# Delta rule over the prompt: where the second key unit of the next head stands on TensorE

## The chip, the cores and the metric

The kernel runs as one program on one core of a Trainium2 chip. The metric is the device time of one execution in microseconds (us). Three runs of the kernel before took 2859.43, 2862.31 and 2866.95 us; their median is 2862.31 us. A change of 0.3% is about 8.6 us.

## The reference

The program is one decoder layer: adaptive norm, one input projection, a gated delta rule, a sliding-window attention, two gates, an output projection and a mixture of experts. The change lies in the delta rule over the 1024 prompt tokens, 8 heads of width 128. The reference computes for each head, in chunks of 64 tokens:

```python
A = where(strict, (k * beta) @ k.T * decay, 0)
L = A + eye(C)
sol = triangular_solve(L, [v * beta, k * beta * exp(gc)])
u, w = sol[..., :DV], sol[..., DV:]
# chunk by chunk, S starts at 0
v_new = u - w @ S
o = q_dec @ S + (q @ k.T * decay) @ v_new
S = S * g_end + k_dec.T @ v_new
```

The q, k and v that enter are columns of one product of the normed input with `w_in`, passed through a causal convolution of four taps, SiLU and (q and k) a norm.

## The kernel before, in words

`delta_prompt` (L422) walks over the eight heads in a hardware loop: seven passes with a next head (`nxt` is true) and a last one without. Here a chunk is 128 tokens, so a head has eight, and they are handled as two groups `g` of four. All eight chunk matrices are inverted before the state is touched.

Projections. Each head needs four projections: q (t = 0), k (1), v (2) and the output gate z (3). One is made in three units of 352 columns, and `project(t, u, half, j)` (L880 to L896) makes half of one unit for head `j`: 12 products, so a unit is 24. The 24 write one PSUM bank: `gd_ps` for units 0 and 2, `gd_pv` for unit 1. Units 0 and 2 first wait until ScalarE has copied out what the bank held before; unit 1 waits only for its weights. The q and k units of head i+1 are made while head i is in its solve, and serve as filling for TensorE.

The solve. VectorE inverts the 16x16 diagonal blocks of all chunks by itself (`solve`, L766), which takes about 7 us. SyncE writes the blocks to a scratch in device memory and reads them back in the layout of whole chunk matrices, `gd_Y` and its transpose `gd_YT`, one group after the other. Three levels follow, `l` = 4, 5 and 6, each of which joins blocks of twice the size:

- TensorE multiplies (`gd_x<-gd_Y,gd_am`, L915; at level 6 `gd_Y,gd_AT`, L984), once for each group. This is the level's first product.
- ScalarE copies the result out of PSUM as `gd_T` (L685, L687).
- TensorE multiplies by `gd_YT` (`gd_x<-gd_T,gd_YT`, L915; at level 6 L1006). This is the second product.
- VectorE subtracts from `gd_Y` (L823; at level 6 from a corner of `gd_YT`, L836).
- For levels 5 and 6 TensorE first turns the new `gd_Y` over (L927) behind the first product, and VectorE copies it to `gd_YT` (L826).

What sets the order. Every engine has its own instruction list, written out by hand, and executes it in order; semaphores join the lists. On TensorE (`body`, L930 on) the list of a head in this stretch is: q unit 0, the turn of k, q units 1 and 2, k unit 0 (the loop over `m`, L968), level 4, the first products of level 5, half of k unit 1, the second products of level 5, the other half of k unit 1, then level 6 with the halves of k unit 2 in the same places, then the products with `gd_k` (L915) and the loop over the chunks, where the z units of the next head are the filling. VectorE has in its list, between the `gd_YT` copies of level 4 and the subtractions of level 5, two taps of the q convolution of the next head (`conv(0, i + 1, 2, CONV)`, L753). ScalarE copies k unit 1 out (L611) behind the two `gd_T` copies of level 5. The last head has no next one, and so no projections in its list.

Of the kernel before, what the change touches and what calls it, by code (L numbers as in the profile page):

```python
# [421 lines left out]
def delta_prompt(nc, c, w_in, gdn_norm, out_state):  # L422
# [10 lines left out]
    with ExitStack() as ctx:  # L433
# [47 lines left out]
        def split_count(t, j):  # L481

            return j * 4 + (RANK[t] + 1)
# [25 lines left out]
        with nc.Block() as block:  # L509
# [365 lines left out]
            def _(pe):  # L875
                def passes(t, n, at):

                    return ((half_of(t)[:, n, :], hh[:, n, at]), (half_of(t)[:, n, :], hl[:, n, at]), (w_r[t][:, n, :], hh[:, n, at]))

                def project(t, u, half, j):  # L880

                    done = (qk_proj, qk_proj, v_proj, z_proj)[t]
                    dst = pp[u % 2] if t == 3 else (pps, pv, pps)[u]
                    dst, at = dst[:, 0:C3], slice(u * C3, (u + 1) * C3)
                    if half == 0:
                        pe.wait_ge(w_low, split_count(t, j))
                        m = t * 3 + u
                        if t < 2 and u != 1:
                            pe.wait_ge(qk_evac, j * 6 + m - u // 2)
                        if t >= 2 and u == 2:  # L890
                            pe.wait_ge(v_evac if t == 2 else z_evac, j * 3 + 1)
                    for n in range(4 * half, 4 * half + 4):
                        for v, (a, b) in enumerate(passes(t, n, at)):
                            last = nc.tensor.matmul(dst, a, b, start=(n == 0 and v == 0), stop=(n == KD - 1 and v == 2))  # L894
                    if half == 1:
                        last.then_inc(done, 1)  # L896
# [15 lines left out]
                def quad(dst, a, b):  # L912
                    for n in range(4):
                        at = slice(n * P, (n + 1) * P)
                        last = nc.tensor.matmul(dst[:, at], a[:, at], b[:, at], start=True, stop=True)  # L915
                    return last

                def turn(dst, a, g):
                    for n in range(4):
                        at = slice((4 * g + n) * P, (4 * g + n + 1) * P)  # L920
                        last = nc.tensor.transpose(dst[:, n * P:(n + 1) * P], a[:, at], c.ident[:])
                    return last

                def turn_tiles(dst, a):
                    for n in range(4):
                        at = slice(n * P, (n + 1) * P)
                        last = nc.tensor.transpose(dst[:, at], a[:, at], c.ident[:])  # L927
                    return last

                def body(i, nxt):  # L930
# [34 lines left out]
                        pe.wait_ge(ats, i * 8 + g * 4 + 4)  # L965
                        turn(X[g][0], y[1], g).then_inc(turned, 1)
                    if nxt:
                        for m in range(1, 4):  # L968
                            for half in range(2):
                                project(m // 3, m % 3, half, i + 1)  # L970
                    for l in (4, 5, 6):
                        for g in range(2):
                            if l == 4:
                                pe.wait_ge(kts, i * 2 + g + 1)
                                pe.wait_ge(y_in[g], i * 32 + 32)
                            else:
                                pe.wait_ge(ys, i * 4 + (l - 5) * 2 + g + 1)
                            if l < 6:
                                pe.wait_ge(lvl, i * 4 + (l - 4) * 2 + g + 1)
                                quad(X[g][0], am[g][l % 2], Y[g]).then_inc(p1, 1)  # L980
                            else:
                                for n in range(4):
                                    lo, hi = slice(n * P, n * P + HP), slice(n * P + HP, (n + 1) * P)
                                    last = nc.tensor.matmul(X[g][0][:, lo], AT[g][0:HP, n * P:(n + 1) * P], Y[g][0:HP, lo], start=True, stop=True)  # L984
                                last.then_inc(p1, 1)
                            if l == 5:
                                pe.wait_ge(qds, i * 4 + g * 2 + 2)
                            if l > 4:
                                turn_tiles(X[g][1], Y[g]).then_inc(yturned, 1)
                        if l == 4:  # L990
                            pe.wait_ge(v_silu, i + 1)
                            pe.wait_ge(capped, i * 8 + 8)
                            for g in range(2):
                                turn(pp[g], y[2], g).then_inc(vturned, 1)
                        elif nxt:
                            project(1, l - 4, 0, i + 1)
                        for g in range(2):
                            pe.wait_ge(t1, i * 6 + (l - 4) * 2 + g + 1)
                            if l > 4:
                                pe.wait_ge(yts, i * 6 + (l - 5) * 2 + g + 1)  # L1000
                            if l < 6:
                                quad(X[g][0], YT[g], T1[g]).then_inc(p2, 1)
                            else:
                                for n in range(4):
                                    lo, hi = slice(n * P, n * P + HP), slice(n * P + HP, (n + 1) * P)
                                    last = nc.tensor.matmul(X[g][1][:, hi], T1[g][HP:P, n * P:(n + 1) * P], YT[g][HP:P, hi], start=True, stop=True)  # L1006
                                last.then_inc(p3, 1)
                        if nxt and l > 4:
                            project(1, l - 4, 1, i + 1)
                    for g in range(2):  # L1010
                        pe.wait_ge(yts, i * 6 + 4 + g + 1)
                        pe.wait_ge(k2s, i * 4 + g * 2 + 2)
# [35 lines left out]
                for t in (1, 3):  # L1048
                    for u in range(3):
                        for half in range(2):  # L1050
                            project(t, u, half, 0)
                heads(body)(pe)


# [1890 lines left out]
```

## Time and profile before

| What | Value |
|---|---|
| median of three runs | 2862.31 us |
| the profiled execution | 2871.59 us, of it a span of 2869.9 us from the first to the last instruction |
| granted TensorE clock, mean of the span | 0.893 of full speed |
| busy share of the span | TensorE products 84%, weight loads 69%, VectorE 56%, ScalarE 39%, GpSimd 14% |
| the delta rule's eight heads | from about 150 to 905 us of the span |

The busy shares are means over stages with different limits, so they say little about one stage. The views to read are the timeline of an engine (start, length, engine, line, what is written and from what, how many alike, and in brackets the idle time before it and what ended that), and the table of stretches, in which the granted clock of TensorE is a column: 1.00 is 2.4 GHz, 0.50 is 1.2 GHz.

### The profile page before, as it was taken

Reading aid. Unit: us, or ns where it says so; the run is one execution under the profiler, and the core shown is the slowest. Engines: PE = TensorE matmul, PEld = TensorE weight load, DVE = VectorE, ACT = ScalarE, POOL = GpSimd, SP = SyncE. Lnnn points to the kernel's source line nnn. Section 1 sums busy time; section 2 is a strip of 40 time slices with the busy share of each in tenths; the row PEclk is TensorE's granted clock in tenths of the full one; section 3 lists DMA queues with packets and bytes.
Section 4 is the critical chain, followed back from the end, with each engine's and each line's share of the span. In section 5 each row is a group of like instructions: output and inputs, shape, how many; then the busy total and the mean of one; then the engine's idle time right before and its main releaser. Section 6 shows DMA issues by size and latency. Waiting matters only on the chain. (4 is left out here: it accounts for less than half of the span.)

```text
span 2869.9 us, 36218 instructions
## 1 busy us (share of the span) xinstructions
PE 2401.0 (84%) x13026; PEld 1976.7 (69%) x13027; DVE 1594.3 (56%) x2079; ACT 1131.5 (39%) x1591; POOL 412.1 (14%) x429
## 2 busy tenths in 40 slices
PE   4789988998885857689996999997885999999990
PEld 2478888888874643554443999997774888888870
DVE  2355666556653311214445555553546988888984
ACT  3233333333331100013334333332323777777773
POOL 1020212021204020002212000002001111111102
PEclk8899999999997757579998999999986999999995
DMA  7511112111203023021101644445427999999965
GB/s 301 178 41 46 33 46 62 46 34 44 62 17 117 15 73 121 30 66 44 44 22 42 228 135 130 137 134 169 141 68 286 392 403 403 405 402 405 405 263 205
DMA packets 315991, 444.58 MB, mean 155 GB/s; under 512 B 56674, under 2 KB 254802, under 8 KB 295875
## 3 DMA queue, kind: packets, MB, share of 16 engines
q1 hardware_dynamic: 294908, 382.11, 38.0%
q0 software_dynamic: 11296, 39.46, 3.7%
q10 hardware_dynamic: 9720, 22.11, 2.0%
q8 instruction: 43, 0.70, 0.1%
q14 instruction: 24, 0.20, 0.0%
HBM read 388.57 MB, written 57.10 MB: 155 GB/s over the span
## 5 line engine op out<-in xcount | busy, mean ns | idle before, releaser
L2554 DVE TENSOR_TENSOR ex_w_r<-ex_w,ex_wh 128x2048 fp32r<-128x2048 f32 x198 | 447.2, 2287 | 61.6 <-ACT ex_wh L2496 61.4
L2496 ACT ACTIVATE ex_wh<-ex_w 128x2048 fp32r<-128x2048 f32 x198 | 379.1, 1917 | 120.3 <-PE ex_up L2451 41.4
L1858 PE MATMUL mg_psum<-mg_xl,mg_wh 128*128 128x352 f32 x768 | 252.9, 329 | 0.0
L1918 DVE TENSOR_TENSOR mg_w_r<-mg_w,mg_wh 128x1024 fp32r<-128x1024 f32 x96 | 134.1, 1402 | 124.4 <-ACT mg_wh L1871 124.2
L1871 ACT ACTIVATE mg_wh<-mg_w 128x1024 fp32r<-128x1024 f32 x96 | 101.4, 1056 | 186.2 <-DVE mg_out L1945 121.5
L1858 PEld LDWEIGHTS mg_psum<-mg_xl,mg_wh 128*128 128x128 f32 x768 | 149.0, 194 | 0.0
L1858 PE MATMUL mg_psum<-hT_r,mg_wh 128*128 128x352 f32 x384 | 127.8, 333 | 19.8 <-DVE mg_w_r L1918 19.8
L894 PE MATMUL gd_ps<-gd_hh,gd_wh 128*128 128x352 f32 x368 | 122.2, 332 | 10.7 <-ACT preS L614 10.7
L1554 PE MATMUL wp_proj_psum<-hT,wp_wq 128*128 128x512 f32 x256 | 116.4, 608 | 14.1 <-DMA wp_wk<-in_w_in_dram 8.9
L1858 PE MATMUL mg_psum<-hT_r,mg_w_r 128*128 128x352 f32 x384 | 125.9, 328 | 0.0
L894 PE MATMUL gd_ps<-gd_hh,gd_w_r 128*128 128x352 f32 x368 | 119.4, 324 | 0.0
L894 PE MATMUL gd_ps<-hT_r,gd_wh 128*128 128x352 f32 x368 | 119.1, 324 | 0.0
L1486 ACT ACTIVATE wp_s<-wp_s,wp_nm 128x256 f32<-128x256 f32 x128 | 63.4, 496 | 128.2 <-DVE wp_nm L1530 128.2
L2451 PE MATMUL ex_gate<-ex_wh,ex_xh 128*128 128x512 f32 x264 | 108.1, 410 | 4.2 <-DVE ex_xl L2563 4.2
L2462 PE MATMUL ex_down<-ex_wh,ex_ah 128*128 128x512 f32 x264 | 107.9, 409 | 2.4 <-DVE ex_al L2567 2.4
L2422 POOL COPY ex_idx<-slot_tokens 128x1 uint32 (+1 forms) x33 | 38.0, 1152 | 499.4 <-PE ex_T L2441 462.2
L2451 PE MATMUL ex_gate<-ex_wh,ex_xl 128*128 128x512 f32 x264 | 105.4, 399 | 0.0
L2462 PE MATMUL ex_down<-ex_w_r,ex_ah 128*128 128x512 f32 x264 | 105.4, 399 | 0.0
L2451 PE MATMUL ex_gate<-ex_w_r,ex_xh 128*128 128x512 f32 x264 | 105.4, 399 | 0.0
L2462 PE MATMUL ex_down<-ex_wh,ex_al 128*128 128x512 f32 x264 | 105.2, 398 | 0.0
L753 DVE SCALAR_TENSOR_TENSOR gd_y<-gd_pre,gd_tw,gd_y 128x1024 f32<-128x1024 f32 x72 | 104.1, 1446 | 1.5
L2451 PE MATMUL ex_up<-ex_wh,ex_xl 128*128 128x512 f32 x264 | 104.8, 397 | 0.0
(611 smaller groups left out, 5980.3 us busy)
## 6 DMA issues: line engine op xcount, KB each, us to landing
ex_w<-in_w_gate_dram SPq DMA_DIRECT2D x66, 1024.0 KB, 8.0
ex_w<-in_w_up_dram SPq DMA_DIRECT2D x66, 1024.0 KB, 7.6
ex_w<-in_w_down_dram SPq DMA_DIRECT2D x66, 1024.0 KB, 8.5
ada_w<-in_w_ada_dram SPq DMA_DIRECT2D x24, 1024.0 KB, 15.6
mg_w<-in_w_in_dram SPq DMA_DIRECT2D x48, 512.0 KB, 3.7
expert_out_scratch<-ex_y ACTq DMA_DIRECT2D x33, 512.0 KB, 7.7
gd_w<-in_w_in_dram SPq DMA_DIRECT2D x32, 512.0 KB, 4.1
mg_w<-in_w_br_gdn_dram SPq DMA_DIRECT2D x24, 512.0 KB, 3.4
```

Of the source, the lines that this page charges most:

```text
L753: nc.vector.scalar_tensor_tensor(y[t][:], pre[:, t, a:a + T], tw[:, t, a:a + 1], y[t][:], ALU.mult, ALU.add).then_inc(out, 1)
L894: last = nc.tensor.matmul(dst, a, b, start=(n == 0 and v == 0), stop=(n == KD - 1 and v == 2))
L1486: last = nc.scalar.activation(s[b][:, g, :], s[b][:, g, :], ACT.Exp, bias=nm[b][:, g:g + 1], accum_out=sm[b][:, g:g + 1])
L1554: last = nc.tensor.matmul(pj[:], a, c.hT[:, m, u * C4:(u + 1) * C4], start=(m == 0), stop=(m == KD - 1))
L1858: last = nc.tensor.matmul(pm[b][q][:, 0:R], a, x, start=(m == 0 and v == 0), stop=(m == KD - 1 and v == 2))
L1871: nc.scalar.activation(wh[q][:], wl[q][:], ACT.Copy).then_inc(w_high, 1)
L1918: nc.vector.tensor_tensor(wl_r[q][:], wl[q][:], wh[q][:].bitcast(F32), ALU.subtract).then_inc(w_low, 1)
L2422: nc.gpsimd.tensor_copy(idx[b][:], c.ids[:, bass.ds(e, 1)]).then_inc(idxs, 1)
L2451: last = nc.tensor.matmul(dst, a, w, start=(v == 0 and m == 0 and first == 0), stop=(v == 2 and m == 3 and first == 4))
L2462: last = nc.tensor.matmul(pd[:, n * FF:(n + 1) * FF], a, w[:, 2 * m + n, :], start=(half == 0 and m == 0 and v == 0), stop=(half == 1 and ...
L2496: nc.scalar.activation(wh[at][:], wl[b][u][:], ACT.Copy).then_inc(w_high, 1)
L2554: nc.vector.tensor_tensor(wl_r[b][u][:], wl[b][u][:], wh[at][:].bitcast(F32), ALU.subtract).then_inc(w_low, 1)
```

## The change

The loop over `m` in front of level 4 runs one step further, and so makes k unit 1 as well. The two halves of k unit 1 are gone from level 5; the halves of k unit 2 stay in level 6. No product is added or removed, and the lists of VectorE, ScalarE, GpSimd and SyncE are the same instruction by instruction.

```diff
                     if nxt:
-                        for m in range(1, 4):
+                        for m in range(1, 5):
                             for half in range(2):
                                 project(m // 3, m % 3, half, i + 1)
...
-                        elif nxt:
-                            project(1, l - 4, 0, i + 1)
+                        elif nxt and l == 6:
+                            project(1, 2, 0, i + 1)
...
-                        if nxt and l > 4:
-                            project(1, l - 4, 1, i + 1)
+                        if nxt and l == 6:
+                            project(1, 2, 1, i + 1)
```

TensorE, in front of level 4 (L975 and L979 are the waits for ScalarE's copy of k and for the first group's blocks; `gd_ps` is the bank of k unit 0, `gd_pv` that of k unit 1; + is new):

```order
 L894 MATMUL gd_ps<-hT_r,gd_wh 128x352
 L894 MATMUL gd_ps<-gd_hh,gd_w_r 128x352
+L894 MATMUL gd_pv<-gd_hh,gd_wh 128x352
+L894 MATMUL gd_pv<-hT_r,gd_wh 128x352
+L894 MATMUL gd_pv<-gd_hh,gd_w_r 128x352
...
 L975 ISA
 L979 REGISTER_ALU
```

All 24 products of k unit 1 now stand ahead of the waits of level 4. TensorE, in level 5 (first product and turn of the second group, second products of both groups, first product of level 6; - is gone):

```order
 L915 MATMUL gd_x<-gd_Y,gd_am 128x128 x4
 L927 MATMUL gd_x<-ident,gd_Y 128x128 x4
-L894 MATMUL gd_pv<-gd_hh,gd_wh 128x352
-L894 MATMUL gd_pv<-hT_r,gd_wh 128x352
-L894 MATMUL gd_pv<-gd_hh,gd_w_r 128x352
...
 L998 REGISTER_ALU
 L915 MATMUL gd_x<-gd_T,gd_YT 128x128 x4
...
 L984 MATMUL gd_x<-gd_Y,gd_AT 128x64 x4
```

Twelve products are gone between the first and the second products, and twelve between the second products and level 6: from the first product of level 5 to the last turn of level 6 TensorE's list now holds nothing that belongs to the next head.

## Rows read from the trace of the kernel before

**Rows 1.** The page: TensorE's busy time, its share of the span, instructions.

```profile
PE 2401.0 (84%) x13026; PEld 1976.7 (69%) x13027; DVE 1594.3 (56%) x2079; ACT 1131.5 (39%) x1591; POOL 412.1 (14%) x429
```

**Rows 2.** Each head's first VectorE instruction: its line's view; its timeline, second head.

```profile
L784 DVE MEMSET gd_S<- x8: 165/165/165, 150.5 to 832.0; 128x128 f32 x8
...
258.66 0.17 DVE L784 MEMSET gd_S<- 128x128 f32 x1
```

**Rows 3.** TensorE's timeline, second head (start us, us, what, idle before it).

```profile
290.24 0.43 PE L894 MATMUL gd_ps<-gd_hh,gd_wh 128*128 128x352 f32 x1 [0.62 <-ACT preS L614]
...
294.06 0.32 PE L894 MATMUL gd_ps<-gd_hh,gd_w_r 128*128 128x352 f32 x1
299.28 2.07 PE L915 MATMUL gd_x<-gd_Y,gd_am 128*128 128x128 f32 x8 [4.90 <-DMA gd_YT<-yt_block_scratch]
301.63 2.07 PE L915 MATMUL gd_x<-gd_Y,gd_am 128*128 128x128 f32 x8 [0.28 <-DMA gd_YT<-yt_block_scratch]
303.49 1.29 PE L921 MATMUL gd_p<-ident,gd_y 128*128 128x128 f32 x8
304.61 1.95 PE L915 MATMUL gd_x<-gd_T,gd_YT 128*128 128x128 f32 x16
306.53 1.15 PE L915 MATMUL gd_x<-gd_Y,gd_am 128*128 128x128 f32 x8
...
308.85 0.60 PE L927 MATMUL gd_x<-ident,gd_Y 128*128 128x128 f32 x4
309.20 0.41 PE L894 MATMUL gd_pv<-gd_hh,gd_wh 128*128 128x352 f32 x1
...
311.23 1.95 PE L915 MATMUL gd_x<-gd_T,gd_YT 128*128 128x128 f32 x16
312.93 0.41 PE L894 MATMUL gd_pv<-gd_hh,gd_wh 128*128 128x352 f32 x1
...
315.04 1.10 PE L984 MATMUL gd_x<-gd_Y,gd_AT 64*128 64x64 f32 x8
```

**Rows 4.** Line L915's view from 190 to 840 us: what ended TensorE's idle time.

```profile
  DMA gd_YT<-yt_block_scratch: 36.4, 13
```

**Rows 5.** VectorE's timeline, levels 4 to 6 of the second head.

```profile
305.71 0.69 DVE L823 TENSOR_TENSOR gd_Y<-gd_Y,gd_x 128x512 f32<-128x512 f32 x1 [2.10 <-PE gd_x L915]
...
309.48 0.69 DVE L826 COPY gd_YT<-gd_x 128x512 f32<-128x512 f32 x1 [0.64 <-PE gd_x L927]
310.09 2.59 DVE L753 SCALAR_TENSOR_TENSOR gd_y<-gd_pre,gd_tw,gd_y 128x1024 f32<-128x1024 f32 x2
312.60 1.29 DVE L823 TENSOR_TENSOR gd_Y<-gd_Y,gd_x 128x512 f32<-128x512 f32 x2
```

**Rows 6.** Stretches, second head: us, busy of each engine, granted clock, DMA share, GB/s.

```profile
294.40:297.10 2.70, 0.00 (x0) 0.00 (x0) 1.58 (x2) 1.41 (x2) 2.70 (x3) 1.00 0.23 39
297.20:303.90 6.70, 4.34 (x18) 4.06 (x19) 6.38 (x4) 0.77 (x2) 6.70 (x5) 0.50 0.48 142
304.10:309.20 5.10, 5.10 (x47) 4.95 (x46) 2.07 (x3) 2.07 (x5) 1.48 (x2) 1.00 0.00 0
...
315.00:318.10 3.10, 3.10 (x25) 2.75 (x25) 0.69 (x1) 1.14 (x3) 0.00 (x0) 1.00 0.00 0
```

**Rows 7.** Stretches of the last head's level 6 and of what follows it.

```profile
878.60:884.20 5.60, 5.60 (x45) 5.06 (x45) 2.83 (x5) 0.76 (x2) 5.60 (x4) 1.00 0.00 0
884.30:887.60 3.30, 3.30 (x18) 3.30 (x17) 0.00 (x0) 1.07 (x2) 3.30 (x2) 0.50 0.03 5
```

**Rows 8.** TensorE's timeline: products with `gd_k`, second head, then last head.

```profile
324.18 1.95 PE L915 MATMUL gd_p<-gd_YT,gd_k 128*128 128x128 f32 x16
...
883.75 3.34 PE L915 MATMUL gd_p<-gd_YT,gd_k 128*128 128x128 f32 x16
```

**Rows 9.** Stretches of the third head's start: a gap, and the products behind it.

```profile
362.10:363.90 1.80, 0.02 (x2) 0.00 (x1) 1.20 (x2) 1.77 (x4) 0.00 (x0) 1.00 0.00 0
363.90:366.50 2.60, 2.60 (x23) 2.60 (x24) 1.12 (x3) 0.52 (x1) 0.00 (x0) 1.00 0.00 0
```

## The prediction

> **What bounds the kernel now.** I read four views, from wide to narrow.
>
> The page first: TensorE's products cover 84% of the span [rows 1]. That is a mean over many stages; the change touches one, so the page gives no price.
>
> Then the heads. Each begins with the same VectorE instruction: the second at 258.66, the eighth at 832.0 [rows 2], so six heads take 573.3 us, 95.56 us each. Heads with a next one are copies of each other, and what one gains or loses counts seven times. All rows below are of the second head.
>
> Then TensorE's timeline [rows 3]. K unit 0 starts at 290.24 and its last product at 294.06. Then TensorE has nothing until 299.28: an idle time of 4.90 us, ended by the landing of the first group's blocks, and 0.28 us more until the second group's. Over the seven heads these waits are 36.4 us [rows 4], 5.2 us a head, so every head has them. From the first product of level 5 (306.53) to level 6 (315.04) the same timeline has no idle time: TensorE goes from work of this head to a half of k unit 1 and back. So TensorE waits in front of level 4, and in level 5 it is itself what everything waits for.
>
> Last the granted clock [rows 6]. It was 1.00 (2.4 GHz) until 297.1, in TensorE's idle time, then 0.50 (1.2 GHz) from 297.2 to 303.9, which is nearly all of level 4's first products, and 1.00 again from 304.1 on.
>
> **Part one: 24 products into the idle time.** Unit 0's first and last products start 3.82 us apart with 23 steps between, 0.166 us a step [rows 3]; 24 steps are 4.0 us. Started where unit 0 ends (294.3) they end near 298.3, and the blocks land at 299.28. About 1.0 us is to spare; the cost is nothing. The cover would be gone if the blocks landed more than 1 us earlier. Nothing in the change moves them: they wait for VectorE's solve and SyncE's four transfers, whose lists are unchanged. The unit's own wait, for its weights, is over before the solve starts, since VectorE's list has the weight split ahead of the solve. Nothing else is queued past.
>
> **Part two: 24 products out of level 5.** The first half held TensorE from 309.20 to 311.23, the second from 312.93 to 315.04: 4.14 us on the path [rows 3]. Not all of it comes back, because two other things are late next.
>
> - The second products need the copies of `gd_YT`. The second copy starts at 309.48 and takes 0.69 us [rows 5], so it ends at 310.17. From a VectorE end to the TensorE instruction that needs it takes 0.13 us: the subtraction ends at 306.40 [rows 5] and the product starts at 306.53 [rows 3]. So the second group's products start at 310.3 instead of about 312.1. All sixteen took 1.70 us (311.23 to 312.93), so these eight end at about 311.15.
> - Level 6 needs the subtraction of level 5, and in front of it VectorE has two convolution taps, from 310.09 to 312.60 [rows 5]. They do not move as long as the copies don't. The two subtractions take 1.29 us, so the first ends at 313.25, and level 6 starts at 313.38 instead of 315.04.
>
> That is 1.66 us a head. TensorE would now stand idle from 311.15 to 313.38, 2.2 us, where it had none. ScalarE's copy-out of unit 1 comes earlier and meets no one. Seven heads: 11.6 us less, if the clock stays as it was.
>
> **Part three: the clock at level 4.** With the unit in the gap, TensorE's longest rest there is 1.0 us, and a second of about 1.3 us between the two groups, since the second group's blocks still land at 301.6. If the clock stays up, the second group's eight products and eight turns, which took 2.98 us (301.63 to 304.61) at 1.2 GHz, take what the same work takes in level 5: eight products 0.99 us at most, and four turns 0.35 us (308.85 to 309.20), so 1.7 us [rows 3]. That saves 1.1 to 1.3 us; I take 1.1. Everything behind, the VectorE taps too, waits for TensorE here and moves with it. Bounds: 0 and 1.3. Together with part two 2.76 us a head, 19.3 us for seven.
>
> **Part four: the clock at level 6.** Here I expect that time to go again. In the last head, which has no projections, level 6 runs from 878.6 to 884.2 with TensorE busy in every record, and the granted clock then was 0.50 from 884.3 to 887.6 [rows 7]. What the engine did before that fall was level 6's thin products (64 rows) and turns, with no projection between them. The same work in the second head, 315.0 to 318.1, stands between two project halves and kept 1.00 [rows 6]. The change takes the half ahead of it away and puts 2.2 us of idle time there. The nearest row on the other side is a rest of 1.8 us at the third head's start, which kept 1.00 [rows 9], but with full products on both sides.
>
> Price: sixteen products with `gd_k` took 1.95 us at 2.4 GHz and 3.34 us in the last head, where most ran at 1.2 GHz [rows 8], so work takes at least 1.7 times as long, and I estimate 1.9. The low stretch lasted 6.8 us at level 4 [rows 6] and 3.4 us in the last head [rows 7]. At 1.9, 6.8 us hold 3.6 us of work and cost 3.2 us; 3.4 us cost 1.6 us. From level 6 to the `gd_k` products TensorE sets the pace, so the loss is on the path. The bounds are 0 (no fall) and 3.2; I take 3.2, from the seven long stretches, because what follows the fall is again thin before the projections return.
>
> A rule speaks the other way. The Trainium skill, page "TensorE: Matmul & The Clock Gate", section "Why this matters for your kernels", ties a drop of throughput in mid-kernel to a long idle gap between bursts of matmuls. The 4.90 us gap agrees with that; the fall at 884.3, with TensorE busy in all records before it, does not. By the rule the clock would stay up in both places, the first rival below.
>
> **The sum.** Per head: -1.66 - 1.1 + 3.2 = +0.44 us, for seven +3.1 us. In some heads the clock will still fall at level 4, since TensorE works only about 1 us there between 298.3 and 301.6; I count two of seven, 1.1 us each, +2.2 us. That is +5.3 us; I say +6. Against the profiled execution (span 2869.9, with what lies around it 2871.59 us) this gives 2877.6; that execution is 9.3 us above the median of the three runs, so against the median, 2862.31, it is 2868 us. The forecast is no change that a measurement tells: 0.3%, or 8.6 us, is about the least that it can tell from none. Its own range is 2864 to 2873.
>
> **The rivals.**
>
> - The clock stays up throughout. For it: the rest of 1.8 us kept 1.00. Against it: the last head's fall. Per head -2.76, so -19.3 us: 2843. Chance 0.12.
> - The clock falls at level 6, but for 3.4 us as in the last head, because the first half of k unit 2 brings it back at once. Per head -2.76 + 1.6 = -1.16, so -8.1 us: 2854. Chance 0.13.
> - Slower: the clock is low at both places. TensorE's little work between 298.3 and 301.6 does not hold it, so part three gives nothing, and level 6 is low as well. Per head -1.66 + 3.2 = +1.54, +10.8 us: 2873, and up to 2877 where the low stretch at level 6 outlasts 6.8 us. It decides from the point where the two rests at level 4 count like one gap: two low stretches a head in place of one. Chance 0.20.
> - The level is bound elsewhere: VectorE's list, with the taps, takes up all that TensorE gives back, or the unit runs into the landing of the blocks. Against it: the 1.0 us to spare and the taps' end at 312.60. About 0 us: 2862. Chance 0.05.
> - The forecast, 2868: chance 0.50.
>
> **How the numbers follow.** Faster by over 0.3% (under 2853.7): the first rival and half of the second, 0.19. Slower by over 0.3% (over 2870.9): the slower rival and about a quarter of the forecast's own range, 0.32. Within 0.3%: the rest, 0.49. The range 2850 to 2876 holds the second rival, the forecast, the fourth and most of the slower one; outside it are the clock that stays up and the far end of the slower case.
>
> **What would show it.** In the changed profile TensorE's wait in front of level 4 falls from 4.9 to about 1 us, without the blocks landing later (part one). Between the second products of level 5 and level 6 a new idle time of about 2.2 us appears, ended by VectorE's subtraction L823 (part two). The table of stretches shows 1.00 across level 4 in most heads (part three) and 0.50 behind level 6's first products for some 7 us (part four). The heads' period goes from 95.56 to 96 us. A period of 92.8 us with 1.00 at level 6 would prove part four wrong, 94.4 its size; a period of 97 us with 0.50 at level 4 proves part three wrong. If the first block's landing moved, part one is wrong.

## The result, and the profile after

The change makes the kernel slower. Its median is 2885.65 us (four runs, 2879.98 to 2887.18) against 2862.84 us for the kernel before on the same chip (four runs, 2859.43 to 2866.95): ratio 1.0070, interval 1.0057 to 1.0083, about 20 us by the ratio (22.8 between the medians). In a later series on one chip it was 2881.95 against 2866.33, ratio 1.0052 (1.0033 to 1.0071). The forecast was 2868, its range ended at 2876, and the time lies outside it on the slow side.

The profiled execution took 2879.98 us, its span is 2878.2. The page first, with the same columns as [rows 1]:

```profile
PE 2422.9 (84%) x13026; PEld 1997.3 (69%) x13027; DVE 1590.8 (55%) x2079; ACT 1130.9 (39%) x1591; POOL 412.4 (14%) x429
```

TensorE runs the same 13026 products and is busy 21.9 us longer (2422.9 - 2401.0). The work didn't grow; the same products took longer. That points to the clock before any wait has been looked at.

Next the heads, as in [rows 2]: VectorE's L784 in the changed kernel, then its timeline at the second and the third head.

```profile
L784 DVE MEMSET gd_S<- x8: 165/165/165, 150.2 to 849.9; 128x128 f32 x8
...
259.95 0.17 DVE L784 MEMSET gd_S<- 128x128 f32 x1
...
358.85 0.17 DVE L784 MEMSET gd_S<- 128x128 f32 x1
```

From the second to the eighth head it is 849.9 - 259.95 = 590.0 us, 98.3 a head where it was 95.56. One head after the other the periods are 109.76, 98.90, 98.89, 98.84, 98.80, 98.76 and 95.78 us (before: 108.18, then 95.52 to 95.59). So each head loses about 3.3 us, but for the first (1.6) and the seventh (0.2). In the profile of the later series the seventh loses as much as the others (98.87 us).

Then TensorE's timeline of the second head (start us, us, what, idle before it), which answers to [rows 3]:

```profile
293.15 0.43 PE L894 MATMUL gd_ps<-gd_hh,gd_wh 128*128 128x352 f32 x1 [0.62 <-ACT preS L614]
...
300.83 0.33 PE L894 MATMUL gd_pv<-gd_hh,gd_w_r 128*128 128x352 f32 x1
302.10 1.15 PE L915 MATMUL gd_x<-gd_Y,gd_am 128*128 128x128 f32 x8 [0.94 <-DMA gd_YT<-yt_block_scratch]
304.51 2.07 PE L915 MATMUL gd_x<-gd_Y,gd_am 128*128 128x128 f32 x8 [1.26 <-DMA gd_YT<-yt_block_scratch]
306.38 1.67 PE L921 MATMUL gd_p<-ident,gd_y 128*128 128x128 f32 x8
307.88 1.95 PE L915 MATMUL gd_x<-gd_T,gd_YT 128*128 128x128 f32 x16
...
312.55 2.17 PE L915 MATMUL gd_x<-gd_T,gd_YT 128*128 128x128 f32 x16
316.61 1.10 PE L984 MATMUL gd_x<-gd_Y,gd_AT 64*128 64x64 f32 x8 [1.89 <-DVE gd_Y L823]
...
328.83 0.38 PE L915 MATMUL gd_p<-gd_YT,gd_k 128*128 128x128 f32 x2
```

The wait in front of level 4 went from 4.90 to 0.94 us, and a new one of 1.89 us stands in front of level 6. Both are as forecast. Cut the head at instants that both kernels have ([rows 2, 3, 8] before, and the start of the third head before):

```profile
354.19 0.17 DVE L784 MEMSET gd_S<- 128x128 f32 x1
```

| stretch of the second head | before | after | difference |
|---|---|---|---|
| head's start to k unit 0 | 31.58 | 33.20 | +1.62 |
| k unit 0 to level 4's first product | 9.04 | 8.95 | -0.09 |
| level 4's first product to its second products | 5.33 | 5.78 | +0.45 |
| from there to level 6 | 10.43 | 8.73 | -1.70 |
| level 6 to the `gd_k` products | 9.14 | 12.22 | +3.08 |
| from there to the next head's start | 30.01 | 30.02 | +0.01 |

The gain of level 5 is there in full. Level 4, where a second gain was expected, lost 0.45 us, and two further losses are larger than what was won: at level 6, as expected, and at the head's start. Where they lie, the stretches show (us, busy of each engine, granted clock, DMA share, GB/s). First level 4 and level 6 of the changed kernel, to be held against [rows 6]:

```profile
297.20:301.10 3.90, 3.90 (x25) 3.65 (x23) 2.77 (x2) 1.41 (x2) 3.90 (x4) 1.00 0.51 132
301.20:304.10 2.90, 1.15 (x8) 0.97 (x8) 2.87 (x3) 0.60 (x1) 2.90 (x2) 1.00 0.65 187
304.30:307.60 3.30, 3.09 (x14) 3.09 (x15) 2.17 (x2) 0.72 (x2) 3.30 (x4) 0.50 0.00 0
307.70:312.00 4.30, 4.30 (x38) 4.15 (x37) 1.96 (x3) 1.56 (x3) 0.74 (x1) 1.00 0.00 0
314.80:316.60 1.80, 0.00 (x0) 0.00 (x0) 1.80 (x3) 0.00 (x0) 0.00 (x0) 1.00 0.00 0
316.60:317.80 1.20, 1.19 (x9) 1.13 (x10) 0.55 (x1) 0.06 (x1) 0.00 (x0) 1.00 0.00 0
317.90:324.70 6.80, 6.80 (x28) 6.21 (x26) 2.51 (x3) 0.60 (x2) 0.00 (x0) 0.50 0.00 0
324.80:330.00 5.20, 5.20 (x40) 5.07 (x40) 0.83 (x2) 0.97 (x3) 0.00 (x0) 1.00 0.00 0
```

Then the second head's start (first three) and the third's (last three), where [rows 9] had 1.00 throughout:

```profile
267.90:269.70 1.80, 0.04 (x1) 0.04 (x1) 1.16 (x2) 1.77 (x4) 0.00 (x0) 1.00 0.00 0
269.70:270.10 0.40, 0.40 (x4) 0.40 (x4) 0.37 (x1) 0.40 (x1) 0.00 (x0) 1.00 0.00 0
270.20:273.50 3.30, 3.30 (x18) 3.30 (x17) 0.54 (x3) 0.00 (x0) 0.00 (x0) 0.50 0.00 0
366.80:368.50 1.70, 0.00 (x0) 0.00 (x0) 1.16 (x2) 1.67 (x4) 0.00 (x0) 1.00 0.00 0
368.60:369.00 0.40, 0.40 (x4) 0.40 (x5) 0.37 (x1) 0.40 (x1) 0.00 (x0) 1.00 0.00 0
369.20:372.40 3.20, 3.20 (x17) 3.20 (x17) 0.53 (x3) 0.00 (x0) 0.00 (x0) 0.50 0.00 0
```

Before, each head had one stretch at 0.50, and TensorE had no work in a third of it (297.2 to 303.9 with 4.34 us busy [rows 6]). Now most heads have three, and TensorE is busy in nearly all of each: 3.4 us at the head's start (the second to the sixth head, and the last), 3.4 us at level 4 (the first six heads), 6.8 us at level 6 (all seven heads with a next one). Read the busy column beside the clock: a low clock costs only what runs under it.

### The profile page after: what moved, and what is told of

It reads as the page before. It is cut to its first block and busy times, and to the rows that moved or that the text cites. A ratio compares the mean times of both kernels' runs of the same rounds, so it can differ in the third digit from the quotient of the medians.

```text
span 2878.2 us, 36218 instructions
## 1 busy us (share of the span) xinstructions
PE 2422.9 (84%) x13026; PEld 1997.3 (69%) x13027; DVE 1590.8 (55%) x2079; ACT 1130.9 (39%) x1591; POOL 412.4 (14%) x429
```

## The experiments

Theory A: level 6 is low because its products are thin and the full-width half ahead of them is gone. Theory B: TensorE's rests, short as they are, bring the clock down, at level 6 and at the other two places. The rival to both: the loss isn't the clock, but VectorE's waits.

The filler in several kernels is one function. Its products go to a bank of PSUM that is overwritten before it is read; they are of no use to the result.

```diff
+                def fill(count):
+                    for n in range(count):
+                        nc.tensor.matmul(X[0][1][:, 0:C3], hh[:, n % KD, 0:P], hh[:, n % KD, 0:C3], start=True, stop=True)
```

**Filler in front of level 6 alone** (against the changed kernel):

```diff
+                        if nxt and l == 5:
+                            fill(12)
                         if nxt and l == 6:
                             project(1, 2, 1, i + 1)
```

> The changed kernel with twelve products of the form of a project half in the idle time between the second products of level 5 and level 6, in the seven heads with a next one. Their result goes to a bank that is overwritten, so they are filling only. Theory (granted clock): the low stretch behind level 6 goes away, 3.1 us a head, and with it most of the low stretch at the next head's start; the period falls from 98.9 to between 94.2 and 95.7 us and the time from 2885.7 to between 2853 and 2864 us. Rival (the loss is a wait on another engine in levels 5 and 6, and the clock only follows it): the filling takes nothing away, 2885 to 2887 us.

Measured: 2860.08 us, ratio 0.9984 (0.9975 to 0.9994) to the kernel before. Level 6 of its second head:

```profile
311.60:317.00 5.40, 5.40 (x38) 4.88 (x39) 3.03 (x4) 0.76 (x2) 0.00 (x0) 1.00 0.00 0
```

Twelve useless products in the idle time take away slightly more than the whole loss. The rival of VectorE's waits falls: VectorE's list is unchanged. The expectation that most of the low stretches at the head's start would go with it was missed: the clock still fell there in five of the seven heads, and at level 4 in six.

**Filler at all three places**, the head's start, ahead of each group of level 4, and level 6:

```diff
+                    if nxt:
+                        pe.wait_ge(v_evac, i * 3 + 1)
+                        for n in range(10):
+                            nc.tensor.matmul(pps[:, 0:C3], hh[:, n % KD, 0:P], hh[:, n % KD, 0:C3], start=True, stop=True)
...
+                                if nxt:
+                                    if g == 0:
+                                        pe.wait_ge(qds, i * 4 + 4)
+                                    fill(5 + g)
...
+                        if nxt and l == 5:
+                            fill(12)
```

> As the run with filling in front of level 6, and five products more in front of level 4, six between the two groups of level 4, and ten in the 1.8 us gap at the head's start. Theory (granted clock): the clock is 1.00 through the whole of the seven heads, and the move is worth what the prediction's parts two and three said, 2.76 us a head against the kernel before: period 92.8 us, time 2843 us. Rival (waits on other engines): 46 us of work more on TensorE in all, time 2885 us or above.

Measured: 2846.81 us, ratio 0.9943 (0.9926 to 0.9959). L784, its timeline at the second head, and the stretch from there to the eighth head:

```profile
L784 DVE MEMSET gd_S<- x8: 165/165/165, 152.4 to 814.3; 128x128 f32 x8
```

```profile
258.96 0.17 DVE L784 MEMSET gd_S<- 128x128 f32 x1
```

```profile
258.96:814.30 555.34, 541.74 (x3632) 505.46 (x3632) 345.15 (x668) 207.48 (x349) 102.35 (x77) 1.00 0.18 48
```

The mean clock over six heads is 1.00, and a head takes 555.34 / 6 = 92.56 us. The prediction had named 92.8 as the period with the clock up. That period is 95.56 us less its parts two and three, so the two were right in size together once the clock was held up, and what the change lost, it lost to the clock.

**Filler at the head's start alone, and at level 4 alone** (the first two edits of the last diff, each by itself). Each was run in two series, in the second beside the changed kernel.

> The changed kernel with ten products as filling in the 1.8 us gap at the start of the seven heads, and nothing else. Theory (three low stretches a head, each with its own price): the low stretch at the head's start goes, which cost 1.6 us in six heads; levels 4 and 6 stay low: period 97.3 us, time 2876 us. Rival (all of it comes from levels 4 to 6, and the stretch at the head's start is not on the path, since VectorE and ScalarE set the pace there): 2884 to 2887 us.

> The changed kernel with five products as filling in front of level 4 and six between its two groups, in the seven heads. Theory (three low stretches a head): level 4 keeps 1.00, which gives the 1.2 us of the prediction's part three back; level 6 and the head's start stay low: time 2877 us. Rival (what is won at level 4 is taken by VectorE's list in level 5): 2884 to 2887 us.

> The changed kernel as it is, on the chip of the three runs beside it, as their reference: 20 us above the kernel before, 2884 to 2887 us, ratio 1.006 to 1.008. If its loss were of one chip alone, it would be within 8 us of the kernel before.

> The changed kernel with ten products of filling in the gap at the head's start, in more rounds. Theory (the stretch at the head's start is one of three that cost time): 9 to 15 us below the changed kernel. Rival (it is not on the path): within 3 us of it.

> The changed kernel with eleven products of filling at level 4, in more rounds. Theory (the stretch at level 4 costs 1.2 us a head): 8 to 13 us below the changed kernel. Rival (VectorE's list takes what is won): within 3 us of it.

Measured first: start 2870.79 us, ratio 1.0005 (0.9979 to 1.0031); level 4 2872.58, ratio 1.0012 (0.9978 to 1.0045). In the second series: the changed kernel 2881.95; start 2869.53, ratio 1.0010 (1.0001 to 1.0020), 12.4 us below the changed kernel; level 4 2868.55, ratio 1.0005 (0.9996 to 1.0014), 13.4 us below it. They were expected to give 9 to 15 and 8 to 13 us. But neither gain is the price of one stretch. With the start filled (second series), level 4 kept 1.00 as well in all seven heads, behind two rests of about 1 us; here the second head from level 4 to the start of level 6, then its level 6:

```profile
301.00:316.00 15.00, 11.36 (x93) 10.57 (x92) 11.64 (x12) 4.02 (x8) 7.22 (x5) 1.00 0.12 36
316.40:323.20 6.80, 6.80 (x28) 6.30 (x27) 2.40 (x3) 0.38 (x1) 0.00 (x0) 0.50 0.00 0
```

With level 4 filled, the start fell in two heads only, and the stretch at level 6 grew from 6.8 to between 10.2 and 13.7 us in four. The periods behind the first head are even with the start filled, 95.33 to 95.77 us; with level 4 filled they go from 94.37 to 98.85. Taking one stretch away moves others.

**Half of the unit in front of level 4, half left in level 5:**

```diff
-                        for m in range(1, 5):
+                        for m in range(1, 4):
...
+                        project(1, 1, 0, i + 1)
...
-                        if nxt and l == 6:
-                            project(1, 2, 1, i + 1)
+                        if nxt and l > 4:
+                            project(1, l - 4, 1, i + 1)
```

> Only the first half of k unit 1 stands in front of level 4; the second half stays between the second products of level 5 and level 6. Theory (granted clock): the 2 us in front of level 6 stay filled, so level 6 keeps 1.00; level 4 is low as in the kernel before; what is won is part two alone, 1.66 us a head: period 93.9 us, time 2851 us. Rival (the work in front of level 4 delays it, or VectorE's list takes the gain): time within 5 us of the kernel before, or in between the two kernels, 2860 to 2875 us.

Measured: 2864.62 us, ratio 0.9999 (0.9989 to 1.0008). The expected 2851 was missed. TensorE's timeline and one stretch of the third head:

```profile
397.39 1.15 PE L915 MATMUL gd_x<-gd_Y,gd_am 128*128 128x128 f32 x8 [3.00 <-DMA gd_YT<-yt_block_scratch]
400.04 2.08 PE L915 MATMUL gd_x<-gd_Y,gd_am 128*128 128x128 f32 x8 [1.50 <-DMA gd_YT<-yt_block_scratch]
...
403.62 3.08 PE L915 MATMUL gd_x<-gd_T,gd_YT 128*128 128x128 f32 x16
```

```profile
399.20:405.90 6.70, 5.86 (x27) 5.86 (x28) 2.81 (x3) 1.79 (x3) 4.46 (x4) 0.50 0.00 1
```

The low stretch is as long as in [rows 6], but begins later in the head: 5.86 us of work lie in it and no longer 4.34, and level 4's second products take 3.08 us where they took 1.95. In this head, filling the front of an idle time pushed the stretch into the work. The head takes 97.27 us, but its start had a low stretch too. The heads whose only low stretch was one of 3.4 us at level 4 take 92.87 to 93.93 us, near the 93.9 that was expected of all. The heads of this kernel came out differently though their lists are the same.

**VectorE's two taps behind the subtractions of level 5.** The changed kernel's TensorE stays as it is; the wait of 1.89 us is taken away by order alone:

```diff
+                        if nxt and l == 5:
+                            conv(0, i + 1, 2, CONV)
...
-                        if nxt:
-                            if l == 4:
-                                conv(0, i + 1, 2, CONV)
-                            else:
-                                low(3, i + 1)
+                        if nxt and l == 5:
+                            low(3, i + 1)
```

> The changed kernel with VectorE's two convolution taps behind the subtractions of level 5 in place of in front of them. TensorE's 1.9 us of idle time in front of level 6 goes, without any filling; the taps now delay level 6's first copy by about 1.1 us. Theory A (the thin products of level 6 alone let the clock fall, as in the last head): level 6 is still followed by a low stretch, 2868 to 2878 us. Theory B (the idle time in front of level 6 makes it fall): 1.00 at level 6, 2855 to 2860 us.

Measured: 2842.84 us, ratio 0.9910 (0.9881 to 0.9939). Third head, TensorE's timeline at level 6, VectorE's, and the stretches (line numbers are one less here):

```profile
404.64 1.10 PE L983 MATMUL gd_x<-gd_Y,gd_AT 64*128 64x64 f32 x8
```

```profile
404.75 0.69 DVE L823 TENSOR_TENSOR gd_Y<-gd_Y,gd_x 128x512 f32<-128x512 f32 x1 [0.42 <-PE gd_x L914]
405.35 2.60 DVE L753 SCALAR_TENSOR_TENSOR gd_y<-gd_pre,gd_tw,gd_y 128x1024 f32<-128x1024 f32 x2
```

```profile
394.30:397.50 3.20, 2.98 (x14) 2.98 (x15) 2.28 (x2) 0.62 (x2) 3.20 (x3) 0.50 0.00 0
...
404.00:408.00 4.00, 4.00 (x33) 3.58 (x32) 3.54 (x5) 0.76 (x2) 0.00 (x0) 1.00 0.00 0
408.00:412.00 4.00, 4.00 (x30) 3.71 (x28) 2.76 (x5) 0.00 (x0) 0.00 (x0) 1.00 0.00 0
```

Level 6 has no idle time in front and keeps 1.00, with no projection half ahead of it either, and so it is in all seven heads. At level 4 (394.3) the clock is still low. Theory A doesn't hold at level 6; the rest in front makes it fall, as theory B says. The other profiles agree: in the six executions that have the rest of 1.89 us there (the changed kernel and the fillings of the head's start alone and of level 4 alone, two executions each) the clock fell behind it in all 42 heads, in the eight executions without it in none of 56. The time lies below theory B's numbers too, since the head's start keeps its clock as well in six of the seven heads, and level 6 starts earlier.

**K unit 2 one place forward.** Here the wait of level 6 is filled with useful work, the first half of k unit 2:

```diff
-                            project(1, 2, 0, i + 1)
+                            project(1, 2, 1, i + 1)
...
-                        if nxt and l == 6:
-                            project(1, 2, 1, i + 1)
+                        if nxt and l == 5:
+                            project(1, 2, 0, i + 1)
```

> As the changed kernel, with k unit 2 one place forward: its first half between the second products of level 5 and level 6, its second half between level 6's first products and its second ones; nothing behind those. Theory (granted clock): no idle time in front of level 6, clock 1.00 there; part two and three are kept, 2.76 us, and the half behind level 6 leaves the path, 2.1 us less a wait of 0.6 us for VectorE: period 91.3 us, time 2833 us; 2841 us if the clock still falls at level 4 in every head. Rival (waits on other engines): VectorE's taps end when they end, level 6 starts no earlier than in the changed kernel, and the time is that of the changed kernel less 1.5 us a head, 2875 us.

> The run with k unit 2 one place forward, with filling in front of level 4 (five products), between its groups (six) and in the gap at the head's start (ten). Theory (clock): the low stretches that were left go, the period is 90.0 us in every head as it was in the heads of that run without a low stretch, time 2826 us. Rival (they are not on the path): 2834 us, as without the filling.

Measured: 2834.08 us, ratio 0.9893 (0.9877 to 0.9910); with filler at level 4 and the head's start as well 2829.92, ratio 0.9862 (0.9795 to 0.9930), a difference inside the intervals. The second head of the version without filler, TensorE's timeline and one stretch:

```profile
294.63 1.15 PE L915 MATMUL gd_x<-gd_Y,gd_am 128*128 128x128 f32 x8 [0.93 <-DMA gd_YT<-yt_block_scratch]
296.83 1.15 PE L915 MATMUL gd_x<-gd_Y,gd_am 128*128 128x128 f32 x8 [1.05 <-DMA gd_YT<-yt_block_scratch]
...
307.42 1.10 PE L984 MATMUL gd_x<-gd_Y,gd_AT 64*128 64x64 f32 x8
```

```profile
292.00:312.00 20.00, 18.02 (x136) 16.70 (x135) 15.25 (x15) 4.82 (x10) 8.93 (x7) 1.00 0.18 51
```

From level 4 to level 6 it takes 12.79 us (changed kernel 14.51), and in this head the clock is 1.00 from end to end. This version beats both kernels without any useless work. The two waits of level 4 are 0.93 and 1.05 us, nearly those of the changed kernel (0.94 and 1.26), where the clock fell. In the third head of this same execution the waits are even shorter in sum, and it did fall:

```profile
384.48 1.15 PE L915 MATMUL gd_x<-gd_Y,gd_am 128*128 128x128 f32 x8 [0.72 <-DMA gd_YT<-yt_block_scratch]
386.71 2.07 PE L915 MATMUL gd_x<-gd_Y,gd_am 128*128 128x128 f32 x8 [1.08 <-DMA gd_YT<-yt_block_scratch]
```

```profile
386.60:390.00 3.40, 3.29 (x15) 3.30 (x16) 2.26 (x2) 0.93 (x2) 3.40 (x4) 0.50 0.00 0
```

It fell at level 4 in three of the seven heads (the third, fourth and seventh), and in the first, with waits of 1.43 and 1.22 us, it did not. So neither the list nor the length of the rests alone decides it there.

**Filler in the kernel before**, 28 products in front of level 4 and 6 between the groups, nothing else changed:

```diff
+                                if nxt:
+                                    if g == 0:
+                                        pe.wait_ge(qds, i * 4 + 4)
+                                    fill(28 if g == 0 else 6)
```

> The kernel before, with nothing moved, and with 28 products of filling in the idle time in front of level 4 and six between its two groups, so that the clock alone is changed there. Theory (part three of the prediction): 1.1 to 1.3 us a head, 8 to 9 us below the kernel before. Rival (level 4's pace is set by the landing of the blocks, and VectorE's list takes what the clock gives): within 3 us of the kernel before.

Measured: 2859.89 us, ratio 0.9979 (0.9969 to 0.9988), 6.0 us below the kernel before where 8 to 9 were expected. Its third head, the start and then level 4:

```profile
361.30:364.70 3.40, 3.40 (x18) 3.40 (x17) 0.93 (x5) 0.00 (x0) 0.00 (x0) 0.50 0.00 0
393.00:397.00 4.00, 3.78 (x29) 3.51 (x30) 3.96 (x3) 1.07 (x2) 4.00 (x3) 1.00 0.27 80
```

The kernel before paid for a low clock all along, about 1 us a head at level 4, as part three said: the second, fifth, sixth and seventh head, now with no low stretch, take 94.17 to 94.80 us where they took 95.5 to 95.6. But in two heads (here 361.3) the start fell instead, which it did in none of the seven before, and these two take 95.93 and 95.89 us. That is the sign, in the opposite kernel, that the stretches trade places. Held against 92.56 us, the period of the changed kernel with filler at all three places, the move itself is worth some 1.9 us a head with the clock up on both sides, near part two's 1.66.

## Why the prediction was wrong, step by step

- **Part one, right.** Unit 1 fits into the idle time: 0.94 us are left of 4.90, as against 1.0 forecast. Over the seven heads the waits of the kind in [rows 4] are now:

```profile
  DMA gd_YT<-yt_block_scratch: 15.0, 14
```

  That is 2.1 us a head, the sum of the two waits, where it was 5.2. Counted from k unit 0 the blocks landed no later (8.95 us, before 9.04).
- **Part two, right.** Level 6 waits for VectorE's subtraction behind two taps, 1.89 us as against 2.2, and from level 4's second products to level 6 the head gained 1.70 us as against 1.66. VectorE's timeline of the second head, which answers to [rows 5]:

```profile
312.75 0.69 DVE L826 COPY gd_YT<-gd_x 128x512 f32<-128x512 f32 x1 [0.64 <-PE gd_x L927]
313.36 2.60 DVE L753 SCALAR_TENSOR_TENSOR gd_y<-gd_pre,gd_tw,gd_y 128x1024 f32<-128x1024 f32 x2
315.87 1.28 DVE L823 TENSOR_TENSOR gd_Y<-gd_Y,gd_x 128x512 f32<-128x512 f32 x2
```

  The kernel with filler at all three places has parts two and three with the clock up: 92.56 us a head, 92.8 forecast. The same kernel as a whole took 2846.81; the first rival, the clock up everywhere, had 2843.
- **Part three, one of two steps that failed.** "In some heads the clock will still fall at level 4 ... I count two of seven." It fell in six of seven (in the later series in all seven), and only at the end of the second wait (304.2), so that 3.09 of 3.30 us were work. The second group's products and turns, which took 2.98 us, took 3.37 (304.51 to 307.88) and not 1.7. So level 4 lost 0.45 us where 1.1 were to be won, and from level 4 to level 6 the head gained 1.25 us and not 2.76. The text held that two short rests of 0.9 and 1.3 us in thin work would mostly be forgiven. Its own slower rival said the opposite; it was the nearest, and still 9 us short of the median.
- **Part four, right in place and size, its reason only in part.** Forecast 6.8 us at 0.50 and +3.2 us a head; found 6.8 us and +3.08. The prediction gave two reasons, thin products without a projection half and the new idle time. The run with VectorE's taps moved kept the thin products, took the idle time away and kept 1.00, so it was the idle time. The fall that spoke for the thin products, in the last head [rows 7], stands in none of the other 13 profiles. The last head of the changed kernel, the same work up to behind its `gd_k` products:

```profile
898.50:907.50 9.00, 8.78 (x70) 7.96 (x68) 3.24 (x6) 1.95 (x4) 9.00 (x5) 1.00 0.01 2
```

- **The missing term, the other step that failed.** The sum has none for the head's start. [Rows 9] had been read as "the rest of 1.8 us kept 1.00", evidence that a rest is harmless. In the changed kernel the same rest and the same products are followed by 0.50:

```profile
269.66 1.70 PE L952 MATMUL gd_x<-gd_y 128*128 128x128 f32 x8 [1.78 <-DVE gd_y L798]
```

  The third head of the kernel before, the same work behind an equal wait:

```profile
363.90 1.16 PE L952 MATMUL gd_x<-gd_y 128*128 128x128 f32 x8 [1.78 <-DVE gd_y L798]
```

  The eight products take 1.70 us now and took 1.16. From the head's start to k unit 0 the second head lost 1.62 us; the stretch stands in five of the seven heads with a next one, and in the last head.

The sum with the measured terms for the second head: +1.62 - 0.09 + 0.45 - 1.70 + 3.08 + 0.01 = +3.4 us, where +0.44 was forecast. Of the 2.9 us between them, part three makes 1.55 and the head's start 1.62; the other terms give back 0.2. The seven periods together are 18.2 us longer (1.58 + 3.37 + 3.37 + 3.29 + 3.24 + 3.17 + 0.19), inside the ratio's interval (0.57% to 0.83% of 2862.84 is 16 to 24 us). Nothing outside these heads is needed. The two profiled spans differ by 8.3 us only (2878.2 - 2869.9), because what follows the eighth head's start, where the change alters no list, took 9.6 us longer in the profiled execution of before (2869.9 - 832.0 = 2037.9, against 2878.2 - 849.9 = 2028.3); that execution was 9.3 us above its median.

The Trainium skill, page "TensorE: Matmul & The Clock Gate", section "Why this matters for your kernels", ties a drop in mid-kernel to a long idle gap between bursts. The trace disagrees: the change took the one long gap away (4.90 us), and the clock fell in three places behind rests of 0.94 to 1.89 us. The rival that went by that rule fails with it.

**What stays open.** Why the rest at the head's start was harmless in one kernel and not in the other, and why level 4's rests were harmless in some heads only. At the start the products, the wait and its length are equal. The list alone doesn't decide it: the seventh head of the changed kernel kept 1.00 at its start and at level 4 in one execution (95.78 us) and in neither place in another (98.87), and in the version with k unit 2 moved level 4 fell in three heads of seven. That it depends on what TensorE did earlier, or on where in time the rest falls, is argued from these pairs; no run shifted a head by a fraction of its period to show it.

## What to carry to other kernels

Moving work into an idle time fills one rest and opens another; before counting the saved products as gain, look up what the engine waits for next and whether that wait stands in front of work that is on the path. A low clock in idle time costs nothing, so price a clock stretch by the busy time that lies in it, and don't take a rest that kept full clock once as proof that it always will. If a new wait appears, fill it with the next useful block or reorder the engine that it waits for: both did more here (2834 and 2843 us) than the change or its reversal.

## What the runs showed of the hardware

- TensorE's granted clock fell to 0.50 behind rests as short as 1.78 us (head's start), and at the end of the second of two, 0.94 and 1.26 us with eight products between them (level 4). It had kept 1.00 through a rest of 1.78 us in the kernel before, and in the version with k unit 2 moved it kept 1.00 behind rests of 0.93 and 1.05 us in one head and fell behind 0.72 and 1.08 us in the next.
- Behind the rest of 1.89 us in front of level 6 it fell in 42 of 42 heads; without the rest, with equally thin products, in none of 56.
- Products of no use in such rests kept the clock at 1.00 over six heads (555.34 us) and made the kernel 31 to 36 us faster than without them (ratio 0.9943 against 1.0052 and 1.0070 to the kernel before).
- The stretches trade places: with level 4 filled in the kernel before, the head's start fell in two heads; the gains of single fillings (12.4 and 13.4 us, and 20 to 25 for level 6 by the ratios) sum to 46 to 51 us, while all three together gave 31 to 36.
